# A hybrid RWKV/PEER layer: routing and row products on VectorE in blocks of sixteen instead of woven together

## The chip, the cores and the metric

The kernel runs on one core of one Trainium2 chip. The metric is the device time of one launch in microseconds, the median of the runs. All arithmetic and all tensors are float32, but for a few one-hot operands in bfloat16.

## The reference

One layer on 256 tokens of width 2048: an RWKV7 scan and a short convolution, a projection back, and then the PEER feed-forward, which is the part that matters here.

```
q = (h @ w_q) -> 8 heads x 2 halves of 128
s1, s2 = q halves @ sub_keys_1, sub_keys_2          # 128 scores each
v1, i1 = top_k(s1, 16);  v2, i2 = top_k(s2, 16)
cand = v1[:, None] + v2[None, :]                    # 256 sums
top, pos = top_k(cand, 16);  eidx = i1*128 + i2 at pos
gate = softmax(top)
act = gelu(h . expert_u[eidx])                      # 128 dots of length 2048 a token
out = sum over 128 of gate * act * expert_v[eidx]
```

With 256 tokens and 8 x 16 chosen experts a token, 32,768 rows of `expert_u` and as many of `expert_v` are wanted.

## The kernel before

Tokens lie on the 128 partitions, in two blocks (`b` = 0, 1). A block has `KTOP` = 128 chosen experts a token, so there are 256 numbers n = 128 b + k; number n means "the k-th expert of each of the 128 tokens of block b".

The dot with `expert_u` is split by columns. The first 896 of the 2048 columns (`KU` = 7 chunks of 128) are multiplied densely on TensorE, for all 16,384 experts, from 128 tiles of 448 KB (`u_dense`, loaded by SyncE into four slots of `u_tile`). ScalarE copies each result of 128 x 256 to `dense` (L761). The other 1152 columns (`GU`) are gathered: for each n GpSimd issues one indirect DMA (`gather`, L544) that fetches 128 rows of 4608 bytes, 590 KB, into one of six slots (`UROWS` = 6, `u_row`). VectorE then makes one product with a sum for each n (`dots`, L1532). A slot is free again when its dot is done: GpSimd waits for `u_dot` of n - 6 before it issues n. The SyncE queue loads tile j when TensorE has finished tile j - 4.

The indices come from routing. `route(b, g)` on VectorE handles two heads of one block: four `top16` of 128 scores, two sums of 16 x 16, two `top16` of 256, and the index arithmetic. It ends in L1510, which raises `picked` and gives GpSimd 32 more numbers. There are 8 such calls (c = 4 b + g). The first runs alone. In the seven others, `between` is called twice in each of the six `top16` and once in each of the two halves of the index arithmetic, 14 times in all, and each time two dots are made: 28 dots in a route, 196 in the seven.

After the last route, `dots(ndot[0], KTOP + LATE)` makes the dots up to n = 223. Then comes the pick stage: 64 groups of four tokens. TensorE (L1175, L1189) selects with a one-hot row the products of each chosen first key from `dense`, and VectorE (`pick`, L1540, four instructions a group) selects the second key. The remaining 32 dots stand there, one behind every second group. TensorE makes group q only when VectorE has finished group q - 2.

Two waits of ScalarE tie its copies to VectorE. The copy of tile 41 (the first that reaches over buffers of the row products; by the sizes of the buffers `dense` begins at 20432, the buffer in question at 31102, and a tile takes 256) waits for `u_dot` = `EARLY` = 48. The copy of tile 112 lands where `scores` lies, and waits for `picked` = 8, that is for the end of the last route. TensorE works in two banks alternately, so it can be at most two tiles ahead of ScalarE.

The dots with n below 48 read their factor from SBUF, the others from PSUM, when `h_ps` says that it is there.

At the end, `expert_v` rows are gathered (12 slots) and VectorE adds them up (L1580), 256 times 2048 columns. That stage begins when the pick stage is over.

Of the kernel before, what the change touches and what calls it, by code (L numbers as in the profile page):

```python
# [54 lines left out]
HEADS, TOPK, NKEYS = 8, 16, 128  # L55
KTOP = HEADS * TOPK
# [43 lines left out]
def build_layer(nc, x, cols, ada, w_in, w_tail, lora_up, keys,  # L100
                u_dense, u_rows, expert_v, out):
    with ExitStack() as ctx:
# [11 lines left out]
        def view(a, *shape):  # L114
            n = int(np.prod(shape))
            v = arena[:, a:a + n]
            if len(shape) == 2:
                v = v.rearrange("p (a b) -> p a b", a=shape[0])
            if len(shape) == 3:
                v = v.rearrange("p (a b c) -> p a b c", a=shape[0], b=shape[1])  # L120
            return v

        def new(*shape):
            return view(take(int(np.prod(shape))), *shape)

        def sem(name):
            return ctx.enter_context(nc.semaphore(name))
# [80 lines left out]
        scores = [view(arena_size - (2 - b) * D, KC, NKEYS) for b in range(TB)]  # L208

        i32 = lambda v: v.bitcast(I32)  # L210
        u32 = lambda v: v.bitcast(U32)
# [8 lines left out]
        v16, i16 = new(2 * 2, TOPK), new(2 * 2, TOPK)  # L220
        iu = new(2 * 2, TOPK)
        repl_at = take(0)
        repl = new(D // 4)
        cand = new(2, TOPK * TOPK)
        hot = [view(repl_at, 4, P), view(repl_at + 4 * P, 4, P)]
        eq = new(2 * TOPK, TOPK)
        topv, pos, hi_u, lo_u, hi_f, lo_f = (new(2, TOPK) for _ in range(6))
# [71 lines left out]
        h_ps = sem("h_rows_ready")  # L299
# [901 lines left out]
        def _(dve):  # L1201
# [221 lines left out]
            for g in range(4):  # L1423
                c = slice(g * GROUP, (g + 1) * GROUP)
# [24 lines left out]
            def r(ins):  # L1449
                nr[0] += 1  # L1450
                return ins.then_inc(vr, 1)

            def settle():
                dve.wait_ge(vr, nr[0])

            NEG = -3.0e38

            def top16(src, vals, where, rep, between):

                r(V.max(vals[:, 0:8], src))  # L1460
                settle()
                r(V.max_index(where[:, 0:8], vals[:, 0:8], src))
                r(V.match_replace(rep, vals[:, 0:8], src, NEG))
                between()
                settle()
                r(V.max(vals[:, 8:16], rep))
                between()
                settle()
                r(V.max_index(where[:, 8:16], vals[:, 8:16], rep))

            def route(b, g, between=lambda: None):

                dve.wait_ge(sc_out, 2 * g + b + 1)
                for c in range(4):
                    top16(scores[b][:, 4 * g + c, :], v16[:, c, :], u32(iu[:, c, :]), repl[:, c * NKEYS:(c + 1) * NKEYS], between)
                settle()
                r(V.tensor_copy(i16[:, :, :], u32(iu[:, :, :])))
                wide = lambda v: v.rearrange("p (a b) -> p a b", b=1).broadcast_to([P, TOPK, TOPK])
                deep = lambda v: v.rearrange("p (a b) -> p a b", a=1).broadcast_to([P, TOPK, TOPK])
                for h in range(2):  # L1480
                    r(tt(cand[:, h, :].rearrange("p (a b) -> p a b", a=TOPK), wide(v16[:, 2 * h, :]), deep(v16[:, 2 * h + 1, :]), ALU.add))
                settle()
                for h in range(2):
                    top16(cand[:, h, :], topv[:, h, :], u32(pos[:, h, :]), repl[:, h * 256:(h + 1) * 256], between)
                settle()
                r(ts(u32(hi_u[:, :, :]), u32(pos[:, :, :]), 4, None, ALU.logical_shift_right))
                r(ts(u32(lo_u[:, :, :]), u32(pos[:, :, :]), 15, None, ALU.bitwise_and))
                settle()
                r(V.tensor_copy(hi_f[:, :, :], u32(hi_u[:, :, :])))
                r(V.tensor_copy(lo_f[:, :, :], u32(lo_u[:, :, :])))  # L1490
                settle()

                gb = gate[:, b, g * 2 * TOPK:(g + 1) * 2 * TOPK].rearrange("p (h k) -> p h k", h=2)
                tt(gb, topv[:, :, :], topv[:, :, 0:1].broadcast_to([P, 2, TOPK]), ALU.subtract).then_inc(gates, 1)

                own = slice(g * 2 * TOPK, (g + 1) * 2 * TOPK)
                for half, sel, dst in ((0, hi_f, idx1f), (1, lo_f, idx2f)):
                    for h in range(2):
                        r(tt(eq[:, h * TOPK:(h + 1) * TOPK, :], wide(sel[:, h, :]), deep(iota16), ALU.is_equal))
                    settle()  # L1500
                    for h in range(2):
                        e = eq[:, h * TOPK:(h + 1) * TOPK, :]
                        r(tt(e, e, deep(i16[:, 2 * h + half, :]), ALU.mult))
                    between()
                    settle()
                    if half:
                        r(V.tensor_copy(idx1_h[b][:, own], idx1f[:, b, own]))
                    r(V.tensor_reduce(dst[:, b, own], eq[:, :, :], AX.X, ALU.add))
                    settle()
                stt(i32(idx[:, b, own]), idx1f[:, b, own], float(NKEYS), idx2f[:, b, own], ALU.mult, ALU.add).then_inc(picked, 1)  # L1510
# [9 lines left out]
                r(tt(gb, gb, grec.rearrange("p (a b) -> p a b", b=1).broadcast_to([P, HEADS, TOPK]), ALU.mult))  # L1520
                settle()

            def dots(lo, hi):

                for n in range(lo, hi):
                    b, k = divmod(n, KTOP)
                    if n == EARLY:
                        dve.wait_ge(h_ps, 1)
                    row = u_row[n % UROWS]
                    dve.wait_ge(u_land[n % UROWS], 16 * (n // UROWS + 1))  # L1530
                    h = junk[:, 0:GU] if n < EARLY else ps[:, b * GU:(b + 1) * GU]
                    stt(row, row, 1.0, h, ALU.mult, ALU.mult, accum_out=actv[:, b, k:k + 1]).then_inc(u_dot, 1)  # L1532

            def pick(q):

                dve.wait_ge(y_ps, q + 1)
                for i in range(4):
                    t = 4 * q + i
                    keyed = bank(5 + q % 2, i * P, (i + 1) * P)
                    stt(keyed, iota, idx2T[:, t:t + 1], keyed, ALU.is_equal, ALU.mult, accum_out=val1T[:, t:t + 1]).then_inc(picked_out, 1)  # L1540

            dve.wait_ge(w_used, WOUT + 16 + 2)
            r(V.tensor_copy(ident_h, ident))
            dve.wait_ge(numbers, 2)
            route(0, 0)
            dve.wait_ge(a2.sem, a2.at("rows"))
            ndot = [0]

            def two_dots():
                dots(ndot[0], ndot[0] + 2)  # L1550
                ndot[0] += 2

            for c in range(1, 8):
                route(c // 4, c % 4, two_dots)
            dots(ndot[0], KTOP + LATE)
            dve.wait_ge(idxT_out, 1)
            for q in range(T // 4):
                pick(q)
                if q % 2:
                    dots(KTOP + LATE + q // 2, KTOP + LATE + q // 2 + 1)  # L1560
            assert LATE + T // 8 == KTOP
            dve.wait_ge(u_dot, TB * KTOP)
            for b in range(TB):
# [3 lines left out]
            for b in range(TB):  # L1567
# [7 lines left out]
                for k in range(KTOP):  # L1575
                    n = b * KTOP + k
# [8 lines left out]
                for h in range(2):  # L1585
                    c = slice(h * D // 2, (h + 1) * D // 2)
# [18 lines left out]
EARLY = 48  # L1605
LATE = KTOP - T // 8
# [62 lines left out]
```

## Time and profile before

| | us |
|---|---|
| median of 3 runs | 2174.09 |
| the runs | 2173.94 to 2176.06 |
| the profiled execution, its own time | 2176.06 |
| its span in the trace | 2174.3 |
| VectorE busy | 1587.0 (73%) |
| TensorE busy | 1401.5 (64%) |
| GpSimd busy | 660.9 (30%) |
| the DMA engines | 313 GB/s over the span |

The stretch that the change touches begins at about 850 us of the span, when the first scores are there, and lasts to about 1503 us, when the pick stage ends. Behind it stands the `expert_v` stage to the end. All times in the rows are microseconds from the start of the span, durations too unless ns is written. A row of the timeline gives start, duration, engine, line, operation, and in brackets how long the engine had been idle and what ended that. The line numbers are those of the kernel before.

### The profile page before, as it was taken

How to read it: one execution, taken by the hardware profiler on the slowest of the kernel's cores; microseconds unless marked ns; L12 is line 12 of the kernel's file. 1: busy time of each engine (PE TensorE's matmuls, PEld its weight loads, DVE VectorE, ACT ScalarE, POOL GpSimd, SP SyncE). 2: the span in 40 equal slices, each digit the busy share in tenths (PEclk: the TensorE clock that was granted, in tenths of full speed). 3: DMA queues.
4: the chain of work that ended last, by engine and by line, in shares of the span. 5: the costliest groups of instructions: out<-in, count | busy, mean ns of one | idle time of the engine just before them, and what ended most of it. 6: DMA issues, size and time to landing. Idle time of an engine off the chain costs nothing.

```text
span 2174.3 us, 20312 instructions
## 1 busy us (share of the span) xinstructions
PE 1401.5 (64%) x7103; PEld 1194.5 (55%) x7103; DVE 1587.0 (73%) x2429; ACT 351.8 (16%) x702; POOL 660.9 (30%) x707
## 2 busy tenths in 40 slices
PE   4899999999998989999999956997000000000000
PEld 3788888888885458888888845896000000000000
DVE  5936555655664023688887888888999998999998
ACT  2032222222221020011111100574000000000000
POOL 1021332123222000454343444323333332333330
PEclk8799999999999999999999987999555555555555
DMA  9946654665455650999999999745999999999995
GB/s 398 384 158 237 232 187 174 236 239 214 164 206 213 251 218 33 369 367 409 410 409 409 407 382 350 255 144 190 422 422 422 421 422 422 423 422 421 422 422 240
DMA packets 122001, 680.99 MB, mean 313 GB/s; under 512 B 13488, under 2 KB 13616, under 8 KB 65840
## 3 DMA queue, kind: packets, MB, share of 16 engines
q0 software_dynamic: 73728, 419.46, 48.1%
q1 hardware_dynamic: 47760, 257.97, 30.8%
q10 hardware_dynamic: 416, 2.25, 0.3%
q8 instruction: 62, 1.02, 0.2%
q14 instruction: 35, 0.29, 0.0%
HBM read 675.44 MB, written 4.19 MB: 313 GB/s over the span
## 4 chain that ended last, share of the span: by engine, by line
PE 40%; DMA 29%; DVE 26%; issue 2%; ACT 1%; POOL 1%; DVEq 0%; ACTq 0%; POOLq 0%
DVE ps L1580 15%; DMA arena<-in_u_rows,arena 14%; DMA arena<-in_expert_v,arena 13%; PE ps L868 13%; PE ps L1189 5%; PE ps L917 5%; DVE arena L1532 4%; PE ps L946 4%; PE ps L1161 2%; DVE arena L1238 2%; PE ps L1087 2%; PE ps L951 2%; DMA arena<-in_ada 1%; POOL arena L544 1%; PE ps L960 1%
## 5 line engine op out<-in xcount | busy, mean ns | idle before, releaser
L1580 DVE SCALAR_TENSOR_TENSOR ps<-arena,ps 128x2048 f32<-128x2048 f32 x256 | 602.8, 2355 | 36.1 <-DMA arena<-in_expert_v,arena 5.7
L1161 PE MATMUL ps<-arena 128*128 128x256 f32 x1792 | 390.1, 381 | 45.6 <-ACT arena L761 45.6
L1161 PEld LDWEIGHTS ps<-arena 128*128 128x128 f32 x1792 | 342.3, 191 | 93.1 <-issue 46.0
L544 POOL DMA_INDIRECT arena<-in_u_rows,arena x256 | 250.5, 978 | 404.7 <-DVE arena L1532 340.4
L544 POOL DMA_INDIRECT arena<-in_expert_v,arena x256 | 240.2, 938 | 410.0 <-DVE ps L1580 379.5
L868 PE MATMUL ps<-arena 128*128 128x256 f32 x1440 | 339.3, 379 | 0.0
L1532 DVE SCALAR_TENSOR_TENSOR arena<-arena,ps 128x1152 f32<-128x1152 f32 x208 | 279.2, 1352 | 68.3 <-DMA arena<-in_u_rows,arena 63.1
L868 PEld LDWEIGHTS ps<-arena 128*128 128x128 f32 x1440 | 262.0, 190 | 29.5
L1217 DVE SCALAR_TENSOR_TENSOR arena<-arena 128x2048 f32<-128x2048 f32 x60 | 142.8, 2380 | 0.0
L655 ACT ACTIVATE arena<-ps 128x512 f32<-128x512 f32 x144 | 81.7, 585 | 295.3 <-PE ps L951 116.7
L1189 PE MATMUL ps<-arena 128*128 128x128 f32 x512 | 124.8, 399 | 2.4 <-issue 2.4
L917 PE MATMUL ps<-arena 128*128 128x512 f32 x256 | 113.7, 597 | 1.5 <-DVE arena L1398 1.5
L761 ACT ACTIVATE arena<-ps 128x256 f32<-128x256 f32 x128 | 49.1, 384 | 388.2 <-PE ps L1161 311.6
L1087 PE MATMUL ps<-arena 128*128 128x256 f32 x512 | 111.3, 379 | 0.0
L1358 DVE TENSOR_TENSOR arena<-ps,arena 128x512 f32<-128x512 f32 x40 | 27.7, 691 | 110.5 <-PE ps L946 110.5
L788 ACT ACTIVATE arena<-ps 128x2048 f32<-128x2048 f32 x2 | 3.8, 1878 | 639.3 <-DVE ps L1580 639.3
L1087 PEld LDWEIGHTS ps<-arena 128*128 128x128 f32 x512 | 96.9, 190 | 13.0
L1189 PEld LDWEIGHTS ps<-arena 128*128 128x128 f32 x512 | 98.6, 205 | 6.8 <-issue 2.8
L946 PE MATMUL ps<-arena 128*128 128x128 f32 x704 | 96.2, 280 | 4.3 <-ACT arena L655 3.1
L946 PEld LDWEIGHTS ps<-arena 128*128 128x128 f32 x704 | 89.0, 191 | 17.9 <-ACT arena L655 8.0
L517 POOL TENSOR_TENSOR arena<-arena 128x512 f32<-128x512 f32 x40 | 61.8, 1547 | 93.0 <-PE ps L946 93.0
L1540 DVE SCALAR_TENSOR_TENSOR ps<-arena,ps 128x128 f32<-128x128 f32 x256 | 74.1, 350 | 15.7 <-PE ps L1189 15.2
(248 smaller groups left out, 1574.2 us busy)
## 6 DMA issues: line engine op xcount, KB each, us to landing
arena<-in_ada SPq DMA_DIRECT2D x96, 1024.0 KB, 4.9
arena<-in_u_dense SPq DMA_DIRECT2D x128, 448.0 KB
arena<-in_w_in SPq DMA_DIRECT2D x45, 1024.0 KB, 6.8
arena<-in_w_tail SPq DMA_DIRECT2D x32, 1024.0 KB, 6.9
arena<-in_w_in SPq DMA_DIRECT2D x12, 512.0 KB, 16.6
arena<-in_u_rows,arena POOLq DMA_INDIRECT x256
arena<-in_expert_v,arena POOLq DMA_INDIRECT x256, 25.2
arena<-in_x ACTq DMA_DIRECT2D x1, 2048.0 KB
```

The lines of the kernel that those rows point to most:

```text
L544: nc.gpsimd.indirect_dma_start(out=row, out_offset=None, in_=table[:, :], in_offset=bass.IndirectOffsetOnAxis(ap=i32(idx[:, b, k:k + 1]), ...
L655: am.done(A(out, in_, func, **kw), name)
L868: last = mm(bank(b, 0, T), w[:, k, :], hT[:, k, :], start=(k == 0), stop=(k == KC - 1))
L917: last = mm(bank(OUT_BANKS[g][b]), yT[:, OUT_K[n], b * P:(b + 1) * P], w, start=(n == 0), stop=(n == KC - 1))
L946: last = mm(bank(b, c * P, c * P + P), l[:, c, :], r[:, c, :], start=True, stop=True)
L1087: last = mm(bank(b0 + s // 2, (s % 2) * T, (s % 2) * T + T), w[:, kk, s * P:(s + 1) * P], h2T[:, k, :], start=(k == 0 and s % 2 == 0), sto ...
L1161: last = mm(bank(5 + j % 2, 0, T), u_tile[j % len(u_tile)][:, k, :], h2T[:, k, :], start=(k == 0), stop=(k == KU - 1))
L1189: last = mm(bank(5 + q % 2, i * P, (i + 1) * P), hot[q % 2][:, i, :], dense[:, :, 4 * q + i], start=True, stop=True)
L1217: ins = stt(dst, ring[:, slot, :], silu_c[:, k:k + 1], dst, ALU.mult, ALU.add)
L1532: stt(row, row, 1.0, h, ALU.mult, ALU.mult, accum_out=actv[:, b, k:k + 1]).then_inc(u_dot, 1)
L1540: stt(keyed, iota, idx2T[:, t:t + 1], keyed, ALU.is_equal, ALU.mult, accum_out=val1T[:, t:t + 1]).then_inc(picked_out, 1)
L1580: stt(sums_ps, v_row[n % len(v_row)], wv[:, b, k:k + 1], sums_ps, ALU.mult, ALU.add).then_inc(v_sum, 1)
```

## The change

`between` goes away. `route` is one uninterrupted run of small instructions, and the dots are made in blocks of 16 ahead of each of the seven later routes. So route c starts when c x 16 dots are done; 112 dots stand ahead of or among the routes where there were 196, and 112 (n = 112 to 223) stand in one block behind the last. The pick stage, the 32 dots in it, the loads, the gathers and their waits on the other engines are as they were. The wait for `h_ps` stands behind the third of these routes, again ahead of n = 48.

```diff
-            def top16(src, vals, where, rep, between):
+            def top16(src, vals, where, rep):
                 r(V.max(vals[:, 0:8], src))
                 settle()
                 r(V.max_index(where[:, 0:8], vals[:, 0:8], src))
                 r(V.match_replace(rep, vals[:, 0:8], src, NEG))
-                between()
                 settle()
                 r(V.max(vals[:, 8:16], rep))
-                between()
                 settle()
                 r(V.max_index(where[:, 8:16], vals[:, 8:16], rep))
...
-            def route(b, g, between=lambda: None):
+            def route(b, g):
...
-                    between()
                     settle()
...
-            def dots(lo, hi):
-                for n in range(lo, hi):
-                    b, k = divmod(n, KTOP)
-                    if n == EARLY:
-                        dve.wait_ge(h_ps, 1)
+            def dots(b, lo, hi):
+                for k in range(lo, hi):
+                    n = b * KTOP + k
...
-            ndot = [0]
-            def two_dots():
-                dots(ndot[0], ndot[0] + 2)
-                ndot[0] += 2
-
             for c in range(1, 8):
-                route(c // 4, c % 4, two_dots)
-            dots(ndot[0], KTOP + LATE)
+                dots(0, (c - 1) * 16, c * 16)
+                route(c // 4, c % 4)
+                if c * 16 == EARLY:
+                    dve.wait_ge(h_ps, 1)
+            dots(0, 7 * 16, KTOP)
+            dots(1, 0, LATE)
             dve.wait_ge(idxT_out, 1)
             for q in range(T // 4):
                 pick(q)
                 if q % 2:
-                    dots(KTOP + LATE + q // 2, KTOP + LATE + q // 2 + 1)
+                    dots(1, LATE + q // 2, LATE + q // 2 + 1)
```

On VectorE, at the end of the first route, this stood before (L1510 is the end of a route, L1532 a dot, L1460 to L1469 the search for the best eight and the next eight):

```order
L1508 TENSOR_REDUCE arena<-arena 128x32
L1510 SCALAR_TENSOR_TENSOR arena<-arena 128x32
L1460 MAX arena<-arena 128x8
L1462 MAX_INDEX arena<-arena 128x8
L1463 MATCH_REPLACE arena<-arena 128x128
L1532 SCALAR_TENSOR_TENSOR arena<-arena 128x1152 x2
```

The second route began at once, with two dots behind its third instruction. Now the same place reads (a dot is L1527, the end of a route L1507):

```order
L1505 TENSOR_REDUCE arena<-arena 128x32
L1507 SCALAR_TENSOR_TENSOR arena<-arena 128x32
L1527 SCALAR_TENSOR_TENSOR arena<-arena 128x1152 x16
L1460 MAX arena<-arena 128x8
L1462 MAX_INDEX arena<-arena 128x8
```

Sixteen dots in a row come ahead of the route, and none in it. At the end of the last route VectorE had:

```order
L1532 SCALAR_TENSOR_TENSOR arena<-arena,ps 128x1152 x2
L1507 CAST arena<-arena 128x32
L1508 TENSOR_REDUCE arena<-arena 128x32
L1510 SCALAR_TENSOR_TENSOR arena<-arena 128x32
L1532 SCALAR_TENSOR_TENSOR arena<-arena,ps 128x1152 x28
L1540 SCALAR_TENSOR_TENSOR ps,arena<-arena,ps 128x128 x8
```

And now:

```order
L1504 CAST arena<-arena 128x32
L1505 TENSOR_REDUCE arena<-arena 128x32
L1507 SCALAR_TENSOR_TENSOR arena<-arena 128x32
L1527 SCALAR_TENSOR_TENSOR arena<-arena,ps 128x1152 x112
L1535 SCALAR_TENSOR_TENSOR ps,arena<-arena,ps 128x128 x8
```

Where 28 dots stood between the last route and the first pick (the rows of x8 are two groups of picks), 112 stand now.

## Rows read from the trace of the kernel before

**Rows 1.** Busy time by stretch: engines with instruction counts, PE clock, DMA share, GB/s.
```profile
866.00:1375.00 509.00, 459.74 (x2154) 404.41 (x2153) 405.29 (x929) 59.75 (x153) 225.13 (x229) 0.95 1.00 390
935.00:1275.00 340.00, 340.00 (x1578) 299.29 (x1577) 276.34 (x650) 43.06 (x112) 142.65 (x147) 1.00 1.02 405
1280.00:1324.00 44.00, 0.00 (x0) 0.00 (x0) 42.10 (x100) 0.00 (x0) 20.94 (x23) 0.53 0.92 331
1324.00:1345.00 21.00, 20.10 (x80) 17.26 (x81) 17.34 (x28) 2.58 (x7) 12.08 (x14) 0.84 0.98 358
```

**Rows 2.** Waits, 820 to 1480: engine, line, releaser, total us, times, longest.
```profile
DVE arena L1532 <- DMA arena<-in_u_rows,arena: 82.7, 101, 2.6
ACT arena L761 <- DVE arena L1510: 50.7, 1, 50.7
PE ps L1161 <- ACT arena L761: 45.6, 1, 45.6
```

**Rows 3.** The chain of waits that ended last: start, duration, what.
```profile
1224.62 12.27 DMA arena<-in_u_rows,arena
...
1324.90 45.47 PE ps L1161 x196
```

**Rows 4.** ScalarE's timeline: copies of tiles 0, 111, 112 and 113, and 127.
```profile
937.85 0.39 ACT L761 ACTIVATE arena<-ps 128x256 f32<-128x256 f32 x1 [4.39 <-PE ps L1161]
...
1273.25 0.39 ACT L761 ACTIVATE arena<-ps 128x256 f32<-128x256 f32 x1 [2.64 <-issue]
1324.37 0.66 ACT L761 ACTIVATE arena<-ps 128x256 f32<-128x256 f32 x2 [50.73 <-DVE arena L1510]
...
1370.40 0.38 ACT L761 ACTIVATE arena<-ps 128x256 f32<-128x256 f32 x1 [2.64 <-PE ps L1161]
```

**Rows 5.** DMA by queue, 940 to 1270 (q0 gathers, q1 tiles): packets, MB, share.
```profile
q0 software_dynamic: 20496, 83.99, 63.6%
q1 hardware_dynamic: 15648, 49.85, 38.4%
```

**Rows 6.** VectorE's timeline: the last dots before the pick stage, and its start.
```profile
1372.28 1.35 DVE L1532 SCALAR_TENSOR_TENSOR arena<-arena,ps 128x1152 f32<-128x1152 f32 x1
...
1373.71 1.36 DVE L1532 SCALAR_TENSOR_TENSOR arena<-arena,ps 128x1152 f32<-128x1152 f32 x1
...
1375.56 0.35 DVE L1540 SCALAR_TENSOR_TENSOR ps<-arena,ps 128x128 f32<-128x128 f32 x1 [0.49 <-issue]
```

**Rows 7.** VectorE's timeline: first and last instruction of the route without dots.
```profile
849.89 0.29 DVE L1460 MAX8 arena<-arena 128x8 f32<-128x128 f32 x1 [23.06 <-ACT arena L752]
...
867.21 0.20 DVE L1510 SCALAR_TENSOR_TENSOR arena<-arena 128x32 int32<-128x32 f32 x1
```

**Rows 8.** DMA by queue, 880 to 910 and 910 to 935.
```profile
q0 software_dynamic: 1638, 6.73, 55.4%
...
q0 software_dynamic: 1905, 7.79, 88.5%
```

**Rows 9.** DMA by queue, 866 to 880.
```profile
q0 software_dynamic: 425, 1.77, 38.7%
```

**Rows 10.** VectorE's timeline in the pick stage: a dot.
```profile
1387.12 1.35 DVE L1532 SCALAR_TENSOR_TENSOR arena<-arena,ps 128x1152 f32<-128x1152 f32 x1
```

**Rows 11.** GpSimd's timeline: the gather that this dot releases.
```profile
1388.75 0.94 POOL L544 DMA_INDIRECT arena<-in_u_rows,arena  x1 [3.09 <-DVE arena L1532]
```

**Rows 12.** Busy time in stretches of 1 us behind that gather.
```profile
1389.00:1390.00 1.00, 1.00 (x8) 0.86 (x7) 0.61 (x6) 0.72 (x1) 0.68 (x1) 1.00 0.00 0
1390.00:1391.00 1.00, 1.00 (x10) 0.97 (x8) 0.93 (x7) 0.69 (x1) 0.00 (x0) 1.00 0.63 83
1391.00:1392.00 1.00, 1.00 (x8) 0.86 (x7) 1.00 (x4) 0.72 (x1) 0.00 (x0) 1.00 0.84 313
1392.00:1393.00 1.00, 1.00 (x10) 0.96 (x8) 1.00 (x7) 0.69 (x1) 0.23 (x1) 1.00 0.48 194
```

**Rows 13.** DMA by queue, 1366 to 1375 and 1290 to 1315: gathers alone.
```profile
q0 software_dynamic: 904, 3.71, 102.2%
...
q0 software_dynamic: 1974, 8.10, 92.3%
```

**Rows 14.** TensorE's timeline: its restart behind the stall.
```profile
1324.90 5.46 PE L1161 MATMUL ps<-arena 128*128 128x256 f32 x12 [45.64 <-ACT arena L761]
```

**Rows 15.** VectorE's timeline: the first pick instruction of the last group.
```profile
1502.51 0.35 DVE L1540 SCALAR_TENSOR_TENSOR ps<-arena,ps 128x128 f32<-128x128 f32 x1 [0.26 <-PE ps L1189]
```

More of the change, by code:

```diff
@@ L1463, in top16 @@
                 r(V.match_replace(rep, vals[:, 0:8], src, NEG))
-                between()
                 settle()
                 r(V.max(vals[:, 8:16], rep))
-                between()
                 settle()
                 r(V.max_index(where[:, 8:16], vals[:, 8:16], rep))
-            def route(b, g, between=lambda: None):
+            def route(b, g):
                 dve.wait_ge(sc_out, 2 * g + b + 1)
                 for c in range(4):
-                    top16(scores[b][:, 4 * g + c, :], v16[:, c, :], u32(iu[:, c, :]), repl[:, c * NKEYS:(c + 1) * NKEYS], between)
+                    top16(scores[b][:, 4 * g + c, :], v16[:, c, :], u32(iu[:, c, :]), repl[:, c * NKEYS:(c + 1) * NKEYS])
                 settle()
@@ L1483, in route @@
                 for h in range(2):
-                    top16(cand[:, h, :], topv[:, h, :], u32(pos[:, h, :]), repl[:, h * 256:(h + 1) * 256], between)
+                    top16(cand[:, h, :], topv[:, h, :], u32(pos[:, h, :]), repl[:, h * 256:(h + 1) * 256])
                 settle()
```

## The prediction

> **What bounds the kernel now.** I read the page first: VectorE is busy 73% of the span and the DMA engines carry 313 GB/s, so no engine bounds the whole. Then the busy time by stretch. From 866 to 1375 us, which is routing, row products and tile products together, the DMA engines are full (share 1.00, 390 GB/s), and from 935 to 1275 the more so (1.02, 405 GB/s) [rows 1]. The waits say the same from VectorE's side: it waited 101 times for a gathered row, 82.7 us in all [rows 2], and the chain of waits runs through gathers of about 12 us each up to 1287 [rows 3]. So the time of this stretch is bytes over bandwidth, as long as something is always asked for.
>
> The second thing to see is one large wait. ScalarE's copy of tile 112 waited 50.7 us for the end of the last route, and TensorE stood behind it for 45.6 us [rows 2, 4]; from 1280 to 1324 it made no matmul [rows 1]. The chain of waits passes there and goes on with 45.47 us of TensorE [rows 3]. That looks like a prize of 45 us for whoever ends routing earlier. It is not: the last dot ahead of the pick stage ended at 1375.07, and the first pick began at 1375.56 [rows 6], while the last tile was copied at 1370.40 [rows 4]. Two chains end within 5 us of each other, and the one of VectorE and the DMA is the later.
>
> **What the change does to TensorE.** Tiles take (1273.25 - 937.85)/111 = 3.02 us each [rows 4]. Tile 112 is due at 1276 and tile 127 at 1273.25 + 16 x 3.02 = 1321.6. Route 7 ends (below) at about 1198, so this wait goes, and so does the stall. The other wait, of tile 41 at 937.85 + 41 x 3.02 = 1062 for 48 dots, is met at about 1000. After 1322 TensorE has nothing to do until the picks start. What is late next is VectorE with its rows.
>
> **What it does to the rows.** Needed numbers:
> - A gathered row block is 128 x 4608 B = 590 KB. Beside the tile stream the gathers got 83.99 MB in 330 us, 254.5 GB/s [rows 5], so 2.31 us a block. Alone they got 3.71 MB in 9 us, 412 GB/s [rows 13], and the last dots stand 1.43 us apart (1372.28, 1373.71) [rows 6].
> - A route without dots in it takes 867.41 - 849.89 = 17.5 us, 17.4 of them to its last start [rows 7]; I take 17.4.
> - A dot lasts 1.35 us and the next starts 1.28 us after it where no row is late (dots woven in before ran at the same pace; their number does not change, so VectorE's own work is the same).
> - Restart: a dot ends at 1388.47 (1387.12 + 1.35), its gather is on GpSimd from 1388.75 to 1389.69, and no byte moves before 1390; the block is through by about 1392.6 [rows 10 to 12]. Between the end of a dot and the flow of bytes lie about 1.8 us, and the ramp of the first block costs perhaps 0.3 more.
>
> Six slots hold 6 x 2.31 = 13.9 us of flow. In the steady stretch VectorE is always waiting for a row, so when the 16th dot ends, 1.35 us of that are already through; the gathers run dry after 12.5 us, while the route lasts 17.4. Then the first slot must be freed by a dot, and the gather must start. One cycle of 16 dots and a route takes: the route 17.4, one dot 1.28, restart 1.8 + 0.3, ten more blocks at 2.31 = 23.1 (six of the sixteen lay ready), and the last dot 1.36: 45.2 us. Without the gap it would be 16 x 2.31 = 37.0. Each cycle loses 8.3 us of the gathers' share.
>
> Start: the gathers got 1.77 MB up to 880 and 6.73 MB from 880 to 910 [rows 8, 9], together 14.4 blocks. The dots may begin here at once (before, they waited for the second route's scores until 880), which gives perhaps one block more by 910. So the 16th dot ends at about 912.5, the first of the seven routes at 929.9, and the flow restarts at 933.0. Until the tile stream begins to draw (938) blocks take 1.43 us: 3.5 of the ten; the other 6.5 take 15.0 us. Dot 31 ends at 954.4. Five cycles of 45.2 bring the start of route 7 to 1180.4, its end to 1197.8 and the restart to 1201.2. By then blocks up to n = 117 have landed.
>
> End: tile 127 is asked for when tile 123 is done (937.85 + 123 x 3.02 = 1309.3) and is in by about 1312. Until then (1312 - 1201.2)/2.31 = 48 blocks; 58 are left, alone, at 1.43: 82.9 us, so the last lands at 1394.9 and its dot ends at 1396.3. Before it was 1375.07: +21.2 us.
>
> As a check by bytes: before, between 910 and 1345, the DMA engines fell short of 412 GB/s by 25 us x 99 (the gathers of [rows 8] moved 313), 340 x 7, 44 x 81 and 21 x 54 [rows 1], in all 9.6 MB. After, six gaps of 8.3 us at 254.5 GB/s and one of about 12 us at 412 are 17.6 MB. The difference is 8.0 MB, 19.5 us. Both ways agree.
>
> **The pick stage.** It took 1502.51 - 1375.07 = 127.4 us from the last dot to its last group, (1502.51 - 1375.56)/63 = 2.015 a group [rows 6, 15]. After, its first two groups are ready early, which saves 1.2 us. But TensorE will have stood for 70 us. At the end of the stall before, the granted clock over the stretch was 0.53 (half is 1.2 GHz), and its first 12 matmuls took 5.46 us where 12/14 of a tile at 2.4 GHz take 2.59 [rows 1, 14]: 2.9 us lost. The sum is +1.7 us. The Trainium skill has the same as a rule (TensorE: Matmul & The Clock Gate, Why this matters for your kernels): idle gaps between bursts bring the array back to half clock. This trace agrees with that, and it costs once. Since the whole gap lies behind the tile products, no other matmul pays.
>
> One page speaks for a longer restart. The Trainium skill (DMA: Bandwidth & Descriptors, Anatomy of one DMA) puts a fixed cost of about 2.0 us on each transfer on top of its bytes over 436 GB/s. For 590 KB that is an estimate of 3.4 us from issue to completion, 4.6 with the 0.94 us on GpSimd and the 0.3 ahead of it; the trace has 4.1 from the end of the dot [rows 10 to 12]. By the page a cycle is 0.5 us longer, and the sum would be 2 us more. The trace's number is used.
>
> **The sum.** +21.2 + 1.7 = +22.9 us. The profiled execution (2176.06, span 2174.3) would become 2199.0; it lies 1.97 above the median, so the median would go from 2174.09 to 2197.0. The `expert_v` stage is not touched and starts only when the pick stage is over, so nothing gives the time back.
>
> **Bounds of the unknown terms.** The restart lag and ramp: at least 0 (cycle 43.1), at most twice mine (47.3). With 0 and no loss of clock the same walk gives +11. With a lag 1 us longer, blocks alone at 1.5 us and the clock loss it gives +33. For the pace of the gathers alone there is a far row: 8.10 MB in 25 us [rows 13], 1.82 us a block. There VectorE had route pieces between the dots and set the pace itself, so I stay with 1.43, the row in which it had none; 1.82 is a rival.
>
> **Rivals.**
> - The routes are hidden, and the freed stall decides (faster). Six slots hold 13.9 us against a route of 17.4, so little is missing; and if the tile stream ran ahead in the gap and gave its share up afterwards, nothing would be lost. Then the blocks behind n = 31 come without a gap: (1312 - 953)/2.31 = 155.4 by the end of the tiles, 36.6 left at 1.43 (52.3 us), the last dot ends at 1365.7, 9.4 earlier, and with the 1.7 of the pick stage the change gives about -8: 2166. A later restart costs 1.43/2.31 = 0.62 of itself at the end, and there are six, so 1 us less in a cycle is worth 3.7 us; the +22.9 become faster than -4.3 at a cycle under 38 us. Against it: TensorE is full at 3.02 us a tile in both cases, and the tile queue moved 49.85 MB in 330 us, no more than TensorE eats [rows 5]; it holds at most four tiles, and cannot bank 8 us in each cycle.
> - Part is hidden and the rest is balanced by the stall: within 0.2%, 2174. It takes a cycle of 38 to 40.
> - The gathers alone are slower than 1.43 in a closed loop, as 1.82: the last 58 blocks take 105.6 us instead of 82.9, +45.6, 2220. For it: six slots only, and each gather waits for a dot. Against it: dot, lag and transfer are 5.5 us, and six blocks at 1.43 are 8.6, so the loop is not the limit.
> - The change doesn't end routing early enough for TensorE: route 7 would have to end after 1276, 78 us later than worked out. It cannot at any cycle in the bounds; I give it nothing.
>
> **How the numbers follow.** The forecast's mechanism within +10 to +32 has 0.74, and 0.08 beyond that for sizes I don't see; faster by the freed stall 0.06; balanced 0.05; the slower loop 0.07. A run of this kernel tells 0.2%, about 4.3 us. Slower has 0.74 + 0.08 + 0.07 = 0.89, same 0.05, faster 0.06. The range 2184 to 2206 holds the first case and leaves out some 0.2 of the rest, mostly on both tails.
>
> **What the profile after would show.** TensorE without a gap from 935 to 1322, the last copy (line L761 before) at about 1322, and no wait of ScalarE for the end of a route. Sixteen dots, then 17.4 us of routing, a period of 45 us, with DMA throughput near 150 GB/s for some 7 us in each. Route 7 over at about 1198. Then from 1312 on 1.43 us a dot at 412 GB/s, TensorE at rest and its clock at half. The first pick at about 1397. If instead the dots stand less than 2.31 us apart behind a gap while tiles flow, the tile queue had banked its share and the first rival is right; if they stand 1.8 apart behind 1312, the third is.

## The result, and the profile after

The changed kernel takes 2209.73 us (2208.21 to 2212.54, 4 runs) against 2174.02 for the kernel before in the same series: a ratio of 1.0166 (95% interval 1.0148 to 1.0183), +35.7 us. Forecast were +22.9 and a range that ended at 2206. The direction and the mechanism were right; what a gap without dots costs was taken too small.

The profiled execution took 2209.84, its span 2208.1, 33.8 more than before. The busy time by stretch (columns as in [rows 1]):

```profile
866.00:1410.00 544.00, 455.36 (x2150) 401.04 (x2148) 416.20 (x925) 62.67 (x157) 221.45 (x228) 0.92 0.93 363
935.00:1275.00 340.00, 340.00 (x1576) 299.05 (x1575) 256.49 (x646) 43.05 (x112) 114.91 (x120) 1.00 0.93 357
1322.00:1410.00 88.00, 2.98 (x18) 2.52 (x16) 83.27 (x125) 2.82 (x4) 57.27 (x61) 0.50 1.02 408
```

From 935 to 1275 the DMA engines moved 357 GB/s where they had moved 405 [rows 1], and GpSimd issued 120 gathers where it had issued 147. The waits, 820 to 1540 (columns as in [rows 2]):

```profile
POOL arena L544 <- DVE arena L1527: 390.3, 221, 17.8
...
DVE arena L1527 <- DMA arena<-in_u_rows,arena: 119.2, 105, 5.8
...
PE ps L1189 <- DVE ps L1535: 86.3, 1, 86.3
```

ScalarE's wait of 50.7 us for the last route and TensorE's of 45.6 [rows 2] are gone. TensorE now waits 86.3 us, but for the first picks, and GpSimd waits up to 17.8 us for a slot: the length of a route. The copy of tile 127, on ScalarE's timeline, against 1370.40 before [rows 4]:

```profile
1317.31 0.39 ACT L761 ACTIVATE arena<-ps 128x256 f32<-128x256 f32 x1 [2.64 <-PE ps L1161]
```

VectorE's timeline at the last dot and the first pick, against 1375.07 and 1375.56 [rows 6], and the first pick instruction of the last group, against 1502.51 [rows 15]:

```profile
1408.70 1.36 DVE L1527 SCALAR_TENSOR_TENSOR arena<-arena,ps 128x1152 f32<-128x1152 f32 x1 [0.27 <-DMA arena<-in_u_rows,arena]
...
1409.98 0.35 DVE L1535 SCALAR_TENSOR_TENSOR ps<-arena,ps 128x128 f32<-128x128 f32 x1
...
1536.15 0.35 DVE L1535 SCALAR_TENSOR_TENSOR ps<-arena,ps 128x128 f32<-128x128 f32 x1 [0.25 <-PE ps L1189]
```

In this execution the work ahead of the change happened to be 4.5 us quicker: the first gather was issued at 863.87, at 868.36 before. Counted from there, the last dot ended after 546.2 us instead of 506.7, +39.5; the pick stage took 1.3 us less; 39.5 - 1.3 - 4.5 makes the 33.8 of the span within 0.1.

One cycle on VectorE's timeline: the last dot of a block (n = 63), the first behind the route (64), the seventh (70), the eighth (71), and the last of that block (79):

```profile
1054.36 1.35 DVE L1527 SCALAR_TENSOR_TENSOR arena<-arena,ps 128x1152 f32<-128x1152 f32 x1 [1.01 <-DMA arena<-in_u_rows,arena]
...
1073.07 1.35 DVE L1527 SCALAR_TENSOR_TENSOR arena<-arena,ps 128x1152 f32<-128x1152 f32 x1
...
1080.72 1.35 DVE L1527 SCALAR_TENSOR_TENSOR arena<-arena,ps 128x1152 f32<-128x1152 f32 x1
...
1082.41 1.36 DVE L1527 SCALAR_TENSOR_TENSOR arena<-arena,ps 128x1152 f32<-128x1152 f32 x1 [0.34 <-DMA arena<-in_u_rows,arena]
...
1102.11 1.36 DVE L1527 SCALAR_TENSOR_TENSOR arena<-arena,ps 128x1152 f32<-128x1152 f32 x1 [0.77 <-DMA arena<-in_u_rows,arena]
```

The gap and the rows that lie ready come as forecast. The cycle lasts 1102.11 - 1054.36 = 47.75 us (48.0 as a mean over the four cycles from n = 47 to 111), where 45.2 were worked out. The DMA engines in that gap:

```profile
1064.00:1067.00 3.00, 3.00 (x16) 2.64 (x15) 2.85 (x10) 0.38 (x1) 0.00 (x0) 1.00 0.92 358
1067.00:1070.00 3.00, 3.00 (x16) 2.64 (x15) 2.81 (x12) 0.38 (x1) 0.00 (x0) 1.00 0.54 178
1070.00:1073.00 3.00, 3.00 (x15) 2.65 (x14) 2.86 (x8) 0.38 (x1) 0.00 (x0) 1.00 0.47 153
1075.00:1077.00 2.00, 2.00 (x11) 1.77 (x10) 2.00 (x5) 0.39 (x1) 1.58 (x2) 1.00 0.45 65
```

Full until the 1060s, then only the tile stream (153 GB/s), until some 2 us behind the end of the first dot.

### The profile page after: what moved, and what is told of

Same layout as the page of the kernel before. It is cut to its first block, busy times and chain, and to the rows that moved or that the text cites. A ratio compares the mean times of both kernels' runs of the same rounds, so it can differ in the third digit from the quotient of the medians.

```text
span 2208.1 us, 20312 instructions
## 1 busy us (share of the span) xinstructions
PE 1393.6 (63%) x7103; PEld 1189.2 (54%) x7103; DVE 1599.6 (72%) x2429; ACT 352.0 (16%) x702; POOL 658.9 (30%) x707
## 4 chain that ended last, share of the span: by engine, by line
PE 38%; DMA 30%; DVE 27%; issue 2%; ACT 1%; POOL 1%; DVEq 0%; ACTq 0%; POOLq 0%
DVE ps L1573 15%; DMA arena<-in_u_rows,arena 15%; PE ps L868 14%; DMA arena<-in_expert_v,arena 13%; PE ps L1189 5%; PE ps L917 5%; PE ps L946 4%; DVE arena L1527 3%; DVE arena L1238 2%; PE ps L1087 2%; PE ps L951 2%; DMA arena<-in_ada 1%; PE ps L960 1%; DVE arena L1467 1%; DVE arena L1462 1%
## 5 line engine op out<-in xcount | busy, mean ns | idle before, releaser
L1527 DVE SCALAR_TENSOR_TENSOR arena<-arena,ps 128x1152 f32<-128x1152 f32 x208 | 279.4, 1355 | 78.8 <-DMA arena<-in_u_rows,arena 74.4
L1189 PE MATMUL ps<-arena 128*128 128x128 f32 x512 | 124.9, 399 | 88.7 <-DVE ps L1535 86.3
L1527 DVE SCALAR_TENSOR_TENSOR arena<-arena 128x1152 f32<-128x1152 f32 x48 | 64.4, 1360 | 45.1 <-DMA arena<-in_u_rows,arena 44.8
```

The source lines that it names most:

```text
L1189: last = mm(bank(5 + q % 2, i * P, (i + 1) * P), hot[q % 2][:, i, :], dense[:, :, 4 * q + i], start=True, stop=True)
```

## The experiments

Theory 1: a route without dots starves the six gather slots; what it costs follows from the length of the gap beyond about 6.5 us (read off the cycles of 48: 48 - 16 x 2.31 = 11, less than 17.4 by 6.5). Theory 2: what costs is that only 112 dots stand ahead of the last route and 112 behind. Theory 3: TensorE standing idle ahead of the picks costs. A ratio below is against the kernel before, run in the same series. All kernels with a schedule of their own use the same few lines, with `AHEAD` dots ahead of each of the seven routes and `AT[i]` at the i-th of the 14 places:

```diff
+            def some_dots():
+                more(AT[call[0] % 14])
+                call[0] += 1
             for c in range(1, 8):
-                route(c // 4, c % 4, two_dots)
+                more(AHEAD)
+                route(c // 4, c % 4, some_dots)
```

**Sixteen dots woven in**

```diff
+            AHEAD, AT = 2, [1] * 14
```

> Sixteen dots for each of the seven later routes, as in the changed kernel, but woven in: two ahead of the route and one at each of the 14 places where the kernel before had two. Theory 1 (a route without dots starves the six gather slots): no stretch without a dot is longer than some 2.5 us, so no gather flow is lost, and routing ends early enough for TensorE. The last dot ahead of the picks comes about 9 us before that of the kernel before: 2163 us (2155 to 2172). Theory 2 (too few dots are made before the last route, so 112 rows are left for a stretch in which VectorE paces them at 1.43 us): the same as the changed kernel, 2210 us. Theory 3 (TensorE idle and half-clocked before the picks costs): also slow, 2200 or more, since TensorE ends its tiles just as early.

Measured 2164.7, ratio 0.9969 (0.9957 to 0.9981); before was 2171.41 in this series, so the gain was 6.7 us, not 11. The same counts of dots as in the changed kernel, 2% faster than it, and faster than the kernel before. Theory 2 falls, and with it theory 3 as an account of the whole: TensorE waits for the first picks here too (40.5 us, half as long as the 86.3 above), and the kernel is no slower for it. That the longer wait costs nothing either is seen in the changed kernel itself, whose pick stage took 1.3 us less than before. The stretch of 935 to 1275:

```profile
935.00:1275.00 340.00, 340.00 (x1577) 299.31 (x1576) 280.99 (x674) 43.43 (x113) 145.77 (x149) 1.00 1.02 408
```

408 GB/s, as full as can be.

**Two halves**

```diff
+            AHEAD, AT = 8, [0] * 8 + [8] + [0] * 5
```

> Sixteen dots a route, eight ahead of it and eight in its middle (behind the first replacement in the fifth top-16 search). Theory 1: the trace of the changed kernel loses 10.9 us of gather flow in a gap of 17.4 us, so the first 6.5 us of a gap are free. Two gaps of about 8.8 us lose 2.3 us each, 4.6 a route instead of 10.9; six routes at 0.62 give 23 us back, the first one some 6 more: 2180 us (2172 to 2188). Theory 2 and theory 3: 2210 us.

Measured 2178.68, 1.0042 (1.0027 to 1.0058); before was 2171.41 in this series, so the forecast of 2180 was hit within 2 us. The size per gap was hit less well. Dots 47 and 111:

```profile
995.36 1.36 DVE L1532 SCALAR_TENSOR_TENSOR arena<-arena 128x1152 f32<-128x1152 f32 x1 [1.31 <-DMA arena<-in_u_rows,arena]
...
1153.59 1.36 DVE L1532 SCALAR_TENSOR_TENSOR arena<-arena,ps 128x1152 f32<-128x1152 f32 x1 [2.10 <-DMA arena<-in_u_rows,arena]
```

A cycle takes 39.6 us, 2.6 more than the 37.0 of the gathers' share, where the expectation had 4.6. So the good total is luck in part.

**Blocks of 28**

```diff
+            AHEAD, AT = 28, [0] * 14
```

> The numbers of the kernel before (28 dots a route, 196 in all, 28 behind the last) but in blocks: 28 ahead of each of the seven routes and none in it. Theory 1: a cycle takes 28 x 2.31 + 10.9 = 75.6 us, the last route ends about 1383 of the span, TensorE stalls some 110 us at tile 112, its last 16 tiles end about 1431 and the last dot about 1437: 2236 us (2220 to 2250), slower than the changed kernel. Theory 2: as the kernel before, 2174 us, since just as many dots stand ahead of the last route.

Measured 2227.81, 1.026 (1.0244 to 1.0276), in the range around 2236 and far from 2174. The first dot behind a route (n = 84, 112):

```profile
1103.62 1.35 DVE L1532 SCALAR_TENSOR_TENSOR arena<-arena,ps 128x1152 f32<-128x1152 f32 x1
...
1179.47 1.35 DVE L1532 SCALAR_TENSOR_TENSOR arena<-arena,ps 128x1152 f32<-128x1152 f32 x1
```

75.85 us, the 75.6 expected. The numbers of dots are those of the kernel before; blocking them alone costs 56 us. And here the stall grows, in the waits:

```profile
ACT arena L761 <- DVE arena L1510: 107.1, 1, 107.1
```

**Routes in pairs**

```diff
             for c in range(1, 8):
-                dots(0, (c - 1) * 16, c * 16)
+                if c % 2:
+                    dots(0, max(c - 2, 0) * 16, c * 16)
                 route(c // 4, c % 4)
-                if c * 16 == EARLY:
+                if c == 3:
                     dve.wait_ge(h_ps, 1)
```

> The changed kernel with routes in pairs: 16 dots, two routes in a row (35 us without a dot), 32 dots, two routes, 32 dots, two routes, 32 dots, one route, then 112 dots. The same 112 and 112. Theory 1: three gaps of 34.9 us lose 28.4 each and one of 17.4 loses 10.9, 96 us against 7 x 10.9 = 76 in the changed kernel; the 20 more count 0.62: 2222 us (2215 to 2230). Theory 2: 2210 us.

Measured 2223.51, 1.0243 (1.0227 to 1.0259), against 1.0166 of the changed kernel: +16 us for longer gaps, where 12 were expected.

**Five slots, changed kernel and kernel before**

```diff
-UROWS = 6
+UROWS = 5
```

> The changed kernel with five gather slots in place of six. Theory 1: one block less lies ready at the end of each route, so each gap costs one block of 2.31 us more, six of them at 0.62 and the first at nearly full weight: about 10 us slower than the changed kernel, 2220 us. Theory 2 (pace of the rows left at the end): five slots still carry 1.43 us a row, so 2210 us.

> The kernel before with five gather slots. Theory 1: with dots woven in no slot waits long, and five blocks in flight still keep the DMA engines full: 2174 to 2178 us. If slots in flight matter by themselves, apart from the gaps, this is as much slower as the changed kernel becomes with five: about 10 us, 2184.

The kernel before lost 0.2% (1.0021, 1.0011 to 1.003), as expected. The changed kernel came to 2237.93, 1.0305 (1.0288 to 1.0321), some 30 us more than with six by the two ratios, not 10. Its dots 47 and 111, and then 195 and 223:

```profile
1014.36 1.36 DVE L1527 SCALAR_TENSOR_TENSOR arena<-arena 128x1152 f32<-128x1152 f32 x1 [1.07 <-DMA arena<-in_u_rows,arena]
...
1216.30 1.35 DVE L1527 SCALAR_TENSOR_TENSOR arena<-arena,ps 128x1152 f32<-128x1152 f32 x1 [1.05 <-DMA arena<-in_u_rows,arena]
...
1390.88 1.36 DVE L1527 SCALAR_TENSOR_TENSOR arena<-arena,ps 128x1152 f32<-128x1152 f32 x1 [0.30 <-DMA arena<-in_u_rows,arena]
...
1436.05 1.36 DVE L1527 SCALAR_TENSOR_TENSOR arena<-arena,ps 128x1152 f32<-128x1152 f32 x1 [0.33 <-DMA arena<-in_u_rows,arena]
```

A cycle takes 50.5 us, 2.4 more, one block, as theory 1 has it. But at the end, with no tile left to load, the gathers need 45.17/28 = 1.61 us a block where six slots gave 1.43 to 1.45. So the way of a slot through dot, issue, transfer and completion takes 5 x 1.61 = 8.1 us in a ring of five, not the 5.5 of the prediction, and six slots at 1.43 (8.6) are only just enough. That was my miss in this expectation. These 8.1 us hold some queueing among the gathers themselves: in the changed kernel's pick stage, where gathers go one at a time, they landed 4.2 to 4.6 us after GpSimd began to issue them. With the dot (1.36) and the 0.3 us to the issue that is 5.9 to 6.3 us.

**Fourteen and twenty woven**

```diff
+            AHEAD, AT = 0, [1] * 14
```

```diff
+            AHEAD, AT = 2, [1, 1, 2] * 4 + [1, 1]
```

> One dot at each of the 14 places and none ahead: 98 dots before the last route ends, 126 behind it. Theory 1: no gap, so the same as with 16 woven (2163 us) within 3 us; the number does not matter once routing ends before tile 112 is due. Theory 2: slower than with 16, since more rows are left for the end.

> Twenty dots a route: two ahead, one at most of the 14 places and two at four of them, 140 before the last route ends. Theory 1: the last route ends at about 864 + 140 x 2.31 = 1190 of the span, still ahead of tile 112, so again 2163 us within 3. Only at about 26 a route would the wait of ScalarE for the last route come back.

Twenty: 2164.78, 0.997 (0.9959 to 0.9981), the same as sixteen. Fourteen: 2168.48, 0.9989 (0.998 to 0.9998), some 4 us behind, just outside the 3 expected. The trace says why. Dots 56 and 70:

```profile
1018.81 1.35 DVE L1532 SCALAR_TENSOR_TENSOR arena<-arena,ps 128x1152 f32<-128x1152 f32 x1
...
1052.44 1.35 DVE L1532 SCALAR_TENSOR_TENSOR arena<-arena,ps 128x1152 f32<-128x1152 f32 x1
```

Fourteen dots and a route take 33.6 us, where the gathers need 14 x 2.31 = 32.3, and from 1000 to 1116 VectorE waits for no row at all. Its own work has become the bound: a woven route takes 15.7 us (worked out with the light tiles below), and 15.7 + 14 x 1.28 = 33.6. With sixteen it is 36.2 against 37.0, and the gathers are the bound again.

**Thirds, and two dots in the middle**

```diff
+            AHEAD, AT = 6, [0] * 6 + [5] + [0] * 3 + [5] + [0] * 3
```

```diff
+            AHEAD, AT = 14, [0] * 8 + [2] + [0] * 5
```

> Sixteen dots a route in three blocks: six ahead, five after a third of the route, five after two thirds. No stretch of routing is longer than 6.5 us. Theory 1 (a gap costs what it has beyond 6.5 us, the number read from the changed kernel's cycles): nothing is lost, so the same as 16 woven one by one, 0.997 of the kernel before. Rival: the free part is shorter, because a gap holds up the six slots from the moment it begins: then it comes out between the woven kernel and the halves, near 1.000.

> Fourteen dots ahead of each route and two in its middle. Theory 1: what a gap costs is slots that nobody frees. Two slots freed in the middle let two more blocks (2 x 2.31 us) flow: 4.6 us less lost in each of six cycles, times 0.62, and some 3 us in the first: 20 us faster than the changed kernel, 1.007 of the kernel before. Rival (the length of the longest stretch without a dot is what counts): as the halves, 1.004.

Thirds: 2167.74, 0.9986 (0.9976 to 0.9996). Nearly free: 402 GB/s from 935 to 1275 against 408 woven. What is left is not the slots' doing. VectorE's wait for rows, 1005 to 1155:

```profile
DVE arena L1532 <- DMA arena<-in_u_rows,arena: 0.2, 1, 0.2
```

A cycle takes 37.7 us there, which is VectorE's own work with unbroken pieces of routing (17.4 + 16 x 1.28 = 37.9), just above the 37.0 of the gathers.

Two in the middle: 2203.24, 1.0148 (1.0131 to 1.0164). This expectation failed: 4 us gained on the changed kernel where I said 20, and the rival (1.004) failed as well. The first dot behind each of two routes (n = 64, 80 here):

```profile
1068.31 1.35 DVE L1532 SCALAR_TENSOR_TENSOR arena<-arena,ps 128x1152 f32<-128x1152 f32 x1
...
1112.74 1.35 DVE L1532 SCALAR_TENSOR_TENSOR arena<-arena,ps 128x1152 f32<-128x1152 f32 x1
```

That cycle takes 44.4 us, and the mean from n = 47 to 111 is 45.1, 2.9 less than with one gap, not 4.6. By that the gain should be some 10 us, and in the profiled executions, counted from the first gather, the last dot did end 9.4 us earlier (536.8 against 546.2). The ratios, each against its own series, give less. The size of this effect stays open between 4 and 10 us.

**Light tiles, in blocks and woven**

```diff
-                sp.dma_start(u_tile[...].rearrange("p a b -> p (a b)"), u_dense[j]).then_inc(...)
+                n = KU * P if j < len(u_tile) else P
+                sp.dma_start(u_tile[...].rearrange("p a b -> p (a b)")[:, 0:n], u_dense[j][:, 0:n]).then_inc(...)
```

> The changed kernel, but of the tiles of u_dense from the fifth on only the first 128 of 896 columns are loaded (TensorE multiplies what is left in the slots from before), so the gathers have the DMA engines nearly to themselves. Theory 1: the gathers then need 1.43 us a block, VectorE is as slow as they are, and after a gap it soon catches up: a cycle takes about 39.5 us instead of 48, the last dot ends about 1326, together with TensorE's tiles: some 84 us faster than the changed kernel, 0.977 of the kernel before. Rival (the cost lies on VectorE itself, in blocks of dots or in unbroken routes): the cycle stays near 48.

> Sixteen dots woven into each route, with the same light tiles. Theory 1: VectorE's own work is the bound, 17.4 + 16 x 1.28 = 37.9 us a cycle; the picks start when TensorE has its tiles, about 1320. Only some 3 to 8 us faster than the light kernel in blocks, where the full tiles made 40: 0.974 of the kernel before. Rival (unbroken routes cost VectorE time): the 40 us remain.

Blocks: 2147.82, 0.989 (0.9874 to 0.9907). Woven: 2123.48, 0.9783 (0.9766 to 0.9799). Each is faster than with the full tiles, so with full tiles the DMA engines are what both wait for. But the difference between them is 24 us, of 43 with full tiles, not 3 to 8. The first dot behind the routes, in blocks (n = 64, 80), and on the other kernel the dots 63 and 79:

```profile
1054.03 1.35 DVE L1528 SCALAR_TENSOR_TENSOR arena<-arena,ps 128x1152 f32<-128x1152 f32 x1
...
1095.11 1.35 DVE L1528 SCALAR_TENSOR_TENSOR arena<-arena,ps 128x1152 f32<-128x1152 f32 x1
```

```profile
1025.25 1.35 DVE L1533 SCALAR_TENSOR_TENSOR arena<-arena,ps 128x1152 f32<-128x1152 f32 x1
...
1061.43 1.35 DVE L1533 SCALAR_TENSOR_TENSOR arena<-arena,ps 128x1152 f32<-128x1152 f32 x1
```

41.08 against 36.18 us. The woven cycle has no wait for a row in it, so with 16 dots at 1.28 woven routing takes 36.18 - 20.4 = 15.7 us of VectorE's time; unbroken it takes 17.4. A route of the light kernel in blocks (columns as in [rows 1]):

```profile
1036.67:1054.03 17.36, 17.36 (x82) 15.30 (x81) 16.37 (x71) 2.30 (x6) 0.94 (x1) 1.00 0.46 173
```

VectorE is busy for 16.37 of the 17.36 us: there is 1.0 us of pauses between the small instructions, which a dot can fill. Where the other 0.7 comes from is not shown. So blocking costs 1.7 us a cycle on VectorE itself, which theory 1 left out and the rival had, though far too large. The other 3.2 are rows that come late behind the gap (a block took 1.5 to 1.6 us there, not 1.43).

## Why the prediction was wrong in size

**What held.** The wait for the last route and TensorE's stall went, and gave no time back by themselves. VectorE with its rows came late next. A gap of 17.4 us per route, seven rows without a wait behind it, tile products at full pace, and then 1.43 us a dot (1.45 as a mean over the last dots): all as worked out. The tail is at that pace (n = 197 and 198):

```profile
1370.88 1.36 DVE L1527 SCALAR_TENSOR_TENSOR arena<-arena,ps 128x1152 f32<-128x1152 f32 x1
...
1372.31 1.36 DVE L1527 SCALAR_TENSOR_TENSOR arena<-arena,ps 128x1152 f32<-128x1152 f32 x1
```

So the rival of a slow loop at 1.82 did not come, nor the one in which the freed stall decides.

**The step that failed** is "Six slots hold 6 x 2.31 = 13.9 us of flow", of which 1.35 us "are already through" when the 16th dot ends, with the "ten more blocks at 2.31" behind the gap, and so the 8.3 us that each cycle loses. It takes for granted that a row block has landed as soon as its own bytes have moved, with nothing of the next ones. The runs show that about one block more has moved by then. Counted from the first gather, in us:

| | forecast | measured |
|---|---|---|
| to the end of dot 15 | 44.1 | 46.7 |
| to the end of dot 31 (first gap) | 41.9 | 49.1 |
| to the end of route 7 (five cycles) | 243.4 | 257.3 |
| to the end of dot 223 | 198.5 | 193.2 |
| sum | 527.9 | 546.2 |

The DMA queues in the gap, from the end of dot 63 (1055.7 to 1067; q0 gathers, q1 tiles), and then from the restart to the landing of block 79 (1076 to 1102.1):

```profile
q0 software_dynamic: 585, 2.37, 52.5%
q1 hardware_dynamic: 650, 2.06, 46.7%
```

```profile
q0 software_dynamic: 1597, 6.57, 65.7%
q1 hardware_dynamic: 1110, 3.58, 34.4%
```

When the sixteenth dot had ended, only 2.37 MB were still to come, 4.0 blocks, not 5.4. After the restart 6.57 MB flowed, 11.1 blocks, until the tenth had landed. So the flow first has to be filled again with about one block, and the ten blocks took 1102.1 - 1076.2 = 25.9 us, 2.59 each, not 2.31, though the DMA engines were full for most of that time. That is the 2.8 us a cycle which were missing (2.5 in this cycle, since the forecast had 0.3 for the ramp; 2.8 as a mean): 5 x 2.8 = 14 of the table's third line.

Whether the blocks share the DMA engines, or a landing is told only while the next block moves, these rows don't tell. The last gather ahead of a gap, with none behind it, landed at 1067.74, 0.6 us after its last bytes at 1067.2, so completion alone is about a quarter of a block. The extra block could have been read before the prediction. The bytes of queue q0 in the kernel before, from 850 to 1115.33, when dot 103 began after a wait for its row:

```profile
q0 software_dynamic: 15196, 62.28, 60.2%
```

That is 105.3 blocks, where 104 were wanted by then.

The other lines of the table have it too. When dot 15 began, at 909.21, 10.11 MB had moved, 17.1 blocks and not 16 (queue q0, from 850), and the block more "by 910" that the prediction hoped for had not come: that is the 2.6 us of the first line.

```profile
q0 software_dynamic: 2457, 10.11, 43.9%
```

In the first gap the restart came 2.8 us after the dot and not 1.8, and the flow up to the landing of block 31 took 26.2 us instead of 20.0, for 6.82 MB, 11.6 blocks instead of ten (queue q0, 932 to 958.3):

```profile
q0 software_dynamic: 1655, 6.82, 68.2%
```

These two make the 7.2 us of the second line; part of the 6.2 is that less of the refill fell ahead of the tile stream. The fourth line gives some back, since 68 blocks and not 58 were left for the stretch in which they cost 1.43 each.

One thing softened the loss. The four blocks left did not take 4 x 2.31 us; the gathers ran dry 11.6 us behind the dot, only 1 us ahead of the 12.5 forecast. In those 11.3 us the tile queue moved 2.06 MB, 182 GB/s where it has 49.85 MB/330 us = 151 [rows 5], and after the restart it moved 3.58 MB in 26.1 us, 137 GB/s. So it did run ahead in the gap and gave that up afterwards, as the first rival had it, but by 0.35 MB, less than one tile, and that is too little to hide a gap. With all bytes counted, a cycle loses 17.4 + 1.3 + 1.9 us without a release of bytes, less 4.0 to 4.2 blocks at 2.31: an estimate of 11, as measured (48.0 - 37.0), and the 6.5 us of theory 1 are 4.1 x 2.31 - 3.2 = 6.3.

Three readings of the prediction were off beside that, and weighed little. From its first to its last start the route of [rows 7] takes 17.3 us, not 17.4. VectorE's own work is not the same woven and in blocks (15.7 against 17.4 us a route). And its 4.1 us from the end of a dot end with the last bytes, while the estimate of 4.6 beside them goes to completion; with the 0.6 us above the two agree, and no longer cycle follows from the difference.

The check by bytes did not catch it, because it used the same 8.3 us. Its two sides were one number in two forms.

**The pick stage.** The granted clock was at 0.50 for the 88 us in which TensorE stood. But its first group of matmuls on the restart, at that clock still, took hardly longer than a later one at 1.00 (TensorE's timeline):

```profile
1411.25 2.10 PE L1189 MATMUL ps<-arena 128*128 128x128 f32 x8 [86.27 <-DVE ps L1535]
...
1415.67 1.95 PE L1189 MATMUL ps<-arena 128*128 128x128 f32 x8
```

And the kernel before had a stretch at half clock at the same place (0.55 from 1375 to 1377), with the same duration:

```profile
1375.67 2.05 PE L1189 MATMUL ps<-arena 128*128 128x128 f32 x8
```

The loss of 2.9 us taken from the tile products [rows 14] did not come, and the stage took 126.1 us instead of 127.4. The rule of the Trainium skill on idle gaps (TensorE: Matmul & The Clock Gate, Why this matters for your kernels) holds for the clock in this trace, but here the clock set no time worth naming.

**The range.** With 18.3 us more up to the last dot and 3.0 less in the picks, +22.9 becomes 38.2, which is what the two profiled executions have from the first gather on (39.5 - 1.3); the medians have 35.7. The 2.5 us between the two lie in the work ahead of the change as far as the profiles tell, which differed by 4.5 us in this pair. The upper bound had been set by a longer restart (+33); that a gap also empties and refills what is under way was in neither bound.

## What to carry to other kernels

Where an engine's work paces a ring of loads, a stretch without a release is free only as far as what is still to move when it begins covers it together with the restart behind it; read what is still to move from the bytes behind the last release, not from slots times the time of one load. Here some 6 us were free (4.1 blocks at 2.31, less 3.2 for the next dot and the restart), and a gap of 17.4 us lost 11. Weave such work finely, with enough of it in each route that the engine's own work does not become the bound (fourteen dots a route were too few), but count separately how much of it must stand ahead of a deadline: sixteen or twenty dots woven into each route, instead of 28, also end the stall and beat the kernel before by 0.3%.

## What the runs showed of the hardware that was not expected

- With six gathers of 590 KB outstanding, about one block more than those landed has moved at each landing: 1.35 us behind a landing that VectorE had waited for, 4.0 blocks were left to move, not 5.4, and behind a gap 11.1 blocks moved until the tenth landed. Completion of a last gather took 0.6 us. Whether the blocks overlap or landings are told late was not tried.
- Gathers with nothing else on the DMA engines took 8.1 us from slot to slot in a ring of five, so five slots gave 1.61 us a block; six gave 1.43 to 1.45. One at a time they landed 4.2 to 4.6 us after their issue began.
- While the gathers ran dry, the tile queue moved 182 GB/s, where it has 151 with the gathers in full flow.
- Dots between dependent small instructions of VectorE cost 1.7 us less for each route than the same dots in a block (15.7 against 17.4 us).
- A group of eight 128 x 128 x 128 float32 matmuls took 2.10 us just after 86 us of rest, at a granted clock of 0.50, and 1.95 soon after at 1.00.
